# Norm transposes placed inside the next tile, and a first chunk cut by columns at two stage borders

## What is computed

```python
# block 1
x = x + jnp.einsum('ble,ed->bld', mixed, w_out[l])
h = rms_norm(x, ffn_norm_g[l])
g = jnp.einsum('bld,df->blf', h, w_gate[l])
u = jnp.einsum('bld,df->blf', h, w_up[l])
x = x + jnp.einsum('blf,fd->bld', jax.nn.silu(g) * u, w_down[l])
# block 2
x = x + gate1 * (o @ w_o)
h2 = _modulate(x, norm2_g, shift2, scale2)      # rms norm, scale, shift
qp = (h @ w_pq)                                 # 8 heads x 2 halves x 128
sc = jnp.einsum("bshpd,hpnd->bshpn", qp, sub_keys)
# top 16 per half, top 16 of the pairs, then experts from peer_u, peer_v
```

## Time and profile before

| | before |
|---|---|
| median of 3 runs | 2701.93 us |
| lowest, highest | 2696.2, 2707.88 us |
| profiled execution | 2702.28 us |
| its span, first to last instruction | 2700.4 us |
| mean granted TensorE clock | 0.976 |
| TensorE / VectorE / ScalarE / GpSimd busy | 94 / 65 / 35 / 14% of the span |

### The profile page before, as it was taken

The page is one execution under the profiler, slowest core; times in us unless marked ns, Lnnn a source line. Parts: engine busy times, 40 slices in busy tenths (PEclk is TensorE's granted clock), DMA queues, the critical chain, the costliest instruction groups (busy, mean ns, idle before and its releaser), DMA issues.

```text
span 2700.4 us, 37751 instructions
## 1 busy us (share of the span) xinstructions
PE 2527.5 (94%) x13685; PEld 2150.7 (80%) x13685; DVE 1754.7 (65%) x3867; ACT 953.9 (35%) x1695; POOL 366.9 (14%) x326
## 2 busy tenths in 40 slices
PE   8998978999998987989998989999999999999998
PEld 6777777777777955784488988898988989899976
DVE  5535556554325545556899957877878787777755
ACT  4334422222223535521154544333333333333332
POOL 1001110110000000100000002332333333232300
PEclk9999979999999988999999999999999999999999
DMA  4110004663221201022024456887787887787754
GB/s 181 63 47 1 1 1 162 228 234 120 92 94 63 79 32 48 1 79 86 8 71 164 172 221 213 302 289 264 271 284 271 286 274 279 270 287 264 262 187 140
DMA packets 123077, 431.40 MB, mean 160 GB/s; under 512 B 11648, under 2 KB 36480, under 8 KB 110736
## 3 DMA queue, kind: packets, MB, share of 16 engines
q1 hardware_dynamic: 74336, 241.20, 25.9%
q0 software_dynamic: 44064, 160.98, 17.2%
q10 hardware_dynamic: 4496, 26.84, 2.5%
HBM read 399.61 MB, written 29.36 MB: 159 GB/s over the span
## 4 chain that ended last, share of the span: by engine, by line
PE 73%; DVE 16%; ACT 3%; issue 3%; DVEq 2%; DMA 1%; ACTq 1%; POOL 0%; SPq 0%
PE ps L2116 16%; PE ps L2089 14%; PE ps L1883 9%; PE ps L1837 7%; PE ps L1753 5%; PE ps L1905 4%; PE ps L2075 3%; PE ps L1818 2%; PE ps L2149 2%; PE ps L2025 2%; DVE r L1608 1%; PE ps L1790 1%; PE ps L2006 1%; DVE big L1665 1%; ACT r L678 1%
## 5 line engine op out<-in xcount | busy, mean ns | idle before, releaser
L2089 PE MATMUL ps<-hd_hi,uT_hi 128*128 128x384 f32 x1024 | 349.9, 342 | 2.3 <-ACT uT_lo L911 2.3
L2089 PE MATMUL ps<-hd_hi,uT_lo 128*128 128x384 f32 x1024 | 346.5, 338 | 0.0
L2089 PE MATMUL ps<-hd_lo,uT_hi 128*128 128x384 f32 x1024 | 346.3, 338 | 0.0
L2116 PE MATMUL ps<-v_hi,ew_hi 128*128 128x512 f32 x768 | 321.6, 419 | 9.6 <-DVE ew_lo L1581 5.3
L2116 PE MATMUL ps<-v_hi,ew_lo 128*128 128x512 f32 x768 | 305.2, 397 | 0.0
L2116 PE MATMUL ps<-v_lo,ew_hi 128*128 128x512 f32 x768 | 303.3, 395 | 0.0
L1561 DVE TENSOR_TENSOR uT_lo<-ps,uT_hi 128x512 fp32r<-128x512 f32 x204 | 140.8, 690 | 171.9 <-ACT uT_hi L884 166.9
L576 POOL DMA_INDIRECT big<-peer_u,r x128 | 144.9, 1132 | 736.0 <-DVE r L1637 437.1
L884 ACT ACTIVATE uT_hi<-ps 128x512 fp32r<-128x512 f32 x256 | 152.4, 596 | 181.6 <-PE ps L2075 181.6
L2089 PEld LDWEIGHTS ps<-hd_hi,uT_hi 128*128 128x128 f32 x1024 | 192.7, 188 | 11.3 <-ACT uT_lo L911 3.0
L2089 PEld LDWEIGHTS ps<-hd_hi,uT_lo 128*128 128x128 f32 x1024 | 192.6, 188 | 11.0
(11 more groups left out here) (338 smaller groups left out, 5238.4 us busy)
## 6 DMA issues: line engine op xcount, KB each, us to landing
big<-wst SPq DMA_DIRECT2D x70, 1024.0 KB, 4.9
r<-peer_u SPq DMA_DIRECT2D x128, 512.0 KB
r<-peer_v SPq DMA_DIRECT2D x128, 512.0 KB
r<-wada POOLq DMA_DIRECT2D x48, 512.0 KB, 4.7
gd<-big ACTq DMA_DIRECT2D x24, 1024.0 KB, 9.2
big<-gd SPq DMA_DIRECT2D x32, 768.0 KB
x<-x_in SPq DMA_DIRECT2D x4, 512.0 KB, 6.6
xd<-x SPq DMA_DIRECT2D x4, 512.0 KB, 9.9
```

Of the source, the lines that this page charges most:

```text
L2089: mm = pe.matmul(ps[:, acc_bank(j), 0:DN], w[:, k, :], h[:, KD // 2 * half + k, :], start=(half == 0 and k == 0 and i == 0), stop=(half == ...
L2116: mm = pe.matmul(ps[:, 2 + 2 * t + half, :], w[:, P * t:P * t + P], vv[:, 512 * half:512 * half + 512], start=(i == 0 and n == 0), stop=(i ...
```

## The change

In `mixed_linear` TensorE issues the transposes of tile t-1 behind the second of tile t's four blocks, and no longer those of tile 3, which go to the stage behind. VectorE's evacuation moves with them, from behind `scaled(t)` to behind the second addition. The halves of chunk W_GU are made earlier, on ScalarE ahead of tile 2's norm and on VectorE ahead of tile 3's additions.

The first chunk of gate/up is computed in four pieces: columns 0 to 383 (tiles 0 to 2) of gate, then tile 3's norm transposes, columns 0 to 383 of up, and, once tile 3 is evacuated, columns 384 to 511 of gate and of up. The first chunk of the query product is cut likewise into its two query tiles, and the h2 transposes come behind it; the first scores follow those.

```diff
@@ ScalarE, mix_and_norm
+                    if t == T - 1 and not first:
+                        high_part(W_GU)
...
-            high_part(W_GU)
             high_part(W_GU + 1)
@@ VectorE, block 1 (block 2: evac moved alike)
                 if t + 1 < T:
                     mixed_low(0, t + 1, h_lo)
+                else:
+                    low_part(W_GU)
                 for n in range(4):
                     v.wait_ge(out_acc, 4 * t + n + 1)
                     xs = x[:, t, 256 * n:256 * n + 256]
                     v.tensor_tensor(xs, xs, ps[:, 4 + n, 0:256], ALU.add).then_inc(out_add, 1)
+                    if t and n == 1:
+                        evac(t - 1)
                 scaled(t)
-                if t:
-                    evac(t - 1)
-            low_part(W_GU)
             evac(T - 1)
@@ TensorE, mixed_linear
-                    if t:
-                        norm(layer, [t - 1], buf)
-                norm(layer, [T - 1], buf)
+                        if t and n == 1:
+                            norm(layer, [t - 1], buf)
@@ TensorE, gate/up
-            pe.wait_ge(ln_hT, 9)
+            def gate_up(f, u, lo, hi):
+
+                w_parts = [w.rearrange("p (k u n) -> p k u n", k=KD, u=2)
+                           for w in (high_of(W_GU + f), w_lo[:, (W_GU + f) % WR, :])]
+                for k in range(KD):
+                    for i, (w, h) in enumerate(passes(w_parts, (h_hi, h_lo))):
+                        mm = pe.matmul(ps[:, 2 * (f % 2) + u, lo:hi], w[:, k, u, :], h[:, k, lo:hi],
+                                       start=(k == 0 and i == 0), stop=(k == KD - 1 and i == 2))
+                return mm
...
+                if f == 0:
+                    pe.wait_ge(ln_hT, 8)
+                    gate_up(0, 0, 0, DN)
+                    norm(1, [T - 1], xn1)
+                    gate_up(0, 1, 0, DN)
+                    pe.wait_ge(ln_hT, 9)
+                    gate_up(0, 0, DN, T * P)
+                    mm = gate_up(0, 1, DN, T * P)
+                else:
+                    gate_up(f, 0, 0, T * P)
+                    mm = gate_up(f, 1, 0, T * P)
@@ TensorE, queries
+            def queries(c, lo, hi):
+
+                wt = ring[:, (W_PQ + c // 2) % WR, :].rearrange("p (k n) -> p k n", k=KD)
+                for k in range(KD):
+                    mm = pe.matmul(ps[:, c % 4, lo:hi], wt[:, k, P * (c % 2):P * (c % 2) + P], hT[:, k, lo:hi],
+                                   start=(k == 0), stop=(k == KD - 1))
+                return mm
+
+            chunk(pe, W_PQ)
+            pe.wait_ge(ln_hT, 16)
+            queries(0, 0, DN)
+            norm(3, [T - 1], xn4)
+            queries(1, 0, DN)
             pe.wait_ge(ln_hT, 17)
+            for c in range(2):
+                queries(c, DN, T * P).then_inc(qp_acc, 1)
+            pe.drain().then_inc(w_used, 1)
             pe.wait_ge(out_add, 8 * T)
             for k in range(KD):
                 mm = pe.transpose(ps[:, 4 + k // 4, P * (k % 4):P * (k % 4) + P], hT[:, k, DT * P:T * P], ident)
             mm.then_inc(h2_tr, 1)
             pe.wait_ge(subk_in_s, 16)
             for c in range(17):
-                if c < 16:
-                    w = W_PQ + c // 2
-                    chunk(pe, w)
+                if 2 <= c < 16:
+                    chunk(pe, W_PQ + c // 2)
```

More of the change, by code:

```diff
@@ L2037, in _ @@
             for c in range(17):
-                if c < 16:
-                    w = W_PQ + c // 2
-                    chunk(pe, w)
+                if 2 <= c < 16:
+                    chunk(pe, W_PQ + c // 2)
                     if c >= 4:
                         pe.wait_ge(qp_ev, c - 3)
[L2043 to L2047, removed]
+                    queries(c, 0, T * P).then_inc(qp_acc, 1)
                     if c % 2:
```

## The result

The median went from 2704.04 us (6 runs, 2696.2 to 2713.63) to 2683.93 us (6 runs, 2678.0 to 2693.49): ratio 0.9929, 95% interval 0.991 to 0.9948. That is 20.1 us less, where 18.0 were forecast. The execution of after that was profiled is the longest of its six: 2693.49 us, span 2691.6. So the spans of the two pages (2700.4 and 2691.6) say little by themselves; the tails must be read by distances within one trace.

A forecast was written before the change was run, and what follows sets the result against it. TensorE, 73% of the chain that ended last, was taken as the bound, idle at the end of both output projections. Gains of 9.0 + 9.0 = 18.0 us from 2702.3 gave 2684.3 us, range 2680 to 2690.

The forecast's parts named there:

- Tail A: First output projection, last addition to first silu: 25.26 us before, 16.3 after with 0.87 for inserted transposes, gain 9.0.
- 48 narrow matmuls at 0.111: Tail A's single-pass matmuls of 128 columns: 5.35 us in all, with bounds of 0.059 and 0.222 us each.
- rival 2: Narrow single-pass matmuls cost as much as two-pass ones, 0.222 us: gain 12.7, time 2689.6 us, chance 0.09.
- 0.25 put down for changes of stream: Tail A: 0.25 us added to the sum for TensorE's changes of stream.
- thinnest margin: Tail A: tile 3's evacuation is over 0.8 us before TensorE comes to the last columns; a miss costs under a microsecond.
- Tail B: Second output projection, last addition to third query tile: 28.71 us before, 19.7 after, gain 9.0.
- new wait: Tail B: TensorE waits 1.7 us ahead of the first scores for ScalarE's evacuations of h2 and query tile 0.
- Then the first scores, 0.9: Tail B: the first scores behind TensorE's wait for ScalarE take 0.9 us.
- Rival 1: Tail B: the wait ahead of the first scores lets the clock fall; gain 15.8, time 2686.5 us, chance 0.15.
- The sum: Both tails together: 9.0 + 9.0 = 18.0 us off 2702.3, giving 2684.3 us, 0.67% less.
- Rival 3: Work behind tail B doesn't move, so half or all of B's gain is lost: 2689 to 2693 us, chance 0.06.
- Rival 4: Transposes and narrow matmuls among wide ones hold the clock at 1.2 GHz in both tails: 2713 us, chance 0.02.

The follow-up runs named there:

- e1: The whole change measured again against the kernel before: 2686.49 us, ratio 0.9922.
- e4: The whole change at the second projection only, nothing at the first, against the kernel before: 2691.14 us, ratio 0.9947.
- e12: The whole change timed a third time, against the kernel before: 2686.22 us against 2704.71, ratio 0.993.
- e5: The whole change plus two unused 512-column matmuls in the gap behind the h2 transposes, against the kernel before: 2679.54 us, ratio 0.9919.
- e7: e6 with the scores of two query tiles taken together behind each odd query tile, against the kernel before: 2677.98 us, ratio 0.9907.
- e6: The whole change with the h2 transposes ahead of the first query chunk's narrow part, against the kernel before: 2679.24 us, ratio 0.9913.

## Why the prediction was right, and where not

**Tail A** was forecast at 16.3 us and measured 15.07 + 0.87 = 15.9. The term that was a choice, 48 narrow matmuls at 0.111, has its row now: 441.38 to 446.58 are 47 steps, 0.111 each. The bounds of 0.059 and 0.222 both fall, and rival 2 with the latter. The Trainium skill ("TensorE: Matmul & The Clock Gate", Back-to-back issue gap) gives about 81 ns for such a matmul; the trace of after doesn't agree for this single-pass stream, 111 ns. The prediction's reason, the same weight load, fits the traces but wasn't tested: weight loads fill all of the narrow single-pass stretch (4.90 of 4.90 us from 441.50) and all of the narrow two-pass one (3.00 of 3.00 from 1212.20). The other 0.4 us is the 0.25 put down for changes of stream, which doesn't show, and a 48th step, 0.11, where 47 lie between the first start and the last. The thinnest margin was right: tile 3's evacuation ended at 440.6, where the next instruction of VectorE starts, and its columns were asked for at 441.38, 0.8 us later. That ScalarE's exponential of crow (a row of inputs loaded by GpSimd) would wait 2.20 us for its transfer wasn't foreseen; it cost nothing, since the silu behind it waited 5.25 us for TensorE anyway.

**Tail B** was forecast at 19.7 and measured 19.55 + 0.87 = 20.4. The new wait is 1.65 us for a forecast 1.7, by the two evacuations that were named. The step that failed is "Then the first scores, 0.9", a cost taken from a row at full clock: start to start they took 1.48 (1218.46 to 1219.94), 0.6 more, and the query tile behind them 1.16 more, which the forecast to the first top-k also lacked.

**Rival 1 is what happened**, though it had 0.15. The chance was read off, where a gap of 1.62 us kept the clock. That row wasn't read too short: the trace of before has the clock at 1.00 from there to 226 us. But it has matmuls and not transposes ahead of its gap. In after a gap of 1.65 us lost the clock, with eight transposes ahead of it, and all four profiles with this gap (after, e1, e4, e12) show it (scores 1.55 to 1.69 us, query tile 8.19 to 8.34). Behind matmuls a gap of 1.71 to 1.75 us kept it in all 14 profiles of the last stage. So length alone doesn't decide; which of the differences does wasn't tried. Its price was forecast at 2.2 us and is 1.7 by e5. The Trainium skill (same page, Part 4: PE-mode transpose) says that transposes don't count as TensorE being busy in the same way; the outcome, 1.69 us for eight scores instead of 1.05, agrees with what it would give; no run here puts matmuls in the transposes' place, so the rule itself isn't tested.

**The sum** of 18.0 is 16.4 where the trace can be read, 9.3 + 7.1, with A 0.3 above its term and B 1.9 below. The median of the first comparison shows 20.1. By the tails alone the time would be 2702.3 - 16.4 = 2685.9, next to rival 1's 2686.5; the three medians are 2683.93, 2686.49 and 2686.22. That the first one fell on 2684.3 almost exactly is partly luck: B's term was 1.9 too good, and low-clock stretches outside the tails made up for it.

**Rival 3** fell: e4 alone passes its gain on, and the distance from first top-k to first v_high is 366.1 us in after, 366.3 in before. But its kind is what stopped e7: there an earlier top-k met an order written for the later one. Rival 4 fell with the granted clock of 1.00 in tail A and in tail B up to 1215.60; its price was also a little low, as 0.32 and 0.213 us aren't twice 0.175 and 0.111, and doubled in full it comes to some 2716 instead of 2713. The moved steps cost nothing beside the 0.87 us per tail, as forecast; no further wait of TensorE of over 0.3 us stands in either tail.

**Open** is why the medians of the changed kernels lie 2 to 8 us further below before than their tails do. The clock of the runs accounts for most of it, and no wait that the change moved does; why some executions lose the clock at a wait where others keep it, and why the changed kernels lose less, wasn't found.

## What to carry to other kernels

When an engine waits for the last tile of a stage, give it the next stage's work for the tiles that are ready: moving the preparation by itself brought 6.1 us here, the split chunk the other 10.3. A short wait that is left on TensorE can cost as much again in clock (1.65 us of waiting and 1.7 of clock), so look for independent work to put beside it, as e6 does. And where an order is written out by hand, follow a gain made at its head to the next engine that keeps the old places: five of e7's 6.9 us, by the distances in the trace, came back only when two activations were moved.

## What the runs showed of the hardware

A wait of 1.65 us behind eight transposes lost the clock in four profiles of four, one of 1.72 us behind matmuls in none of 14, and one of 2.28 us in some and not in others. In after it still stood at 1.00 (2.4 GHz) over the wait and fell to 0.50 (1.2 GHz) in the work behind it (1218.90 to 1222.00), so a glance at the wait's own slice of the page would have missed it.

Single-pass matmuls hardly get cheaper below 256 columns. The timeline of TensorE in e12 has single-pass matmuls of 256 columns at the end of the second projection, 1195.19 to 1195.55 in three steps of 0.12:

```profile
1195.19 0.28 PE L1839 MATMUL ps<-w_lo,h_hi 128*128 128x256 f32 x1
1195.30 0.28 PE L1839 MATMUL ps<-h_lo,mid 128*128 128x256 f32 x1
1195.42 0.28 PE L1839 MATMUL ps<-h_lo,h_hi 128*128 128x256 f32 x1
1195.55 0.29 PE L1839 MATMUL ps<-w_lo,h_hi 128*128 128x256 f32 x1
```

At 128 columns it is 0.111. An undivided one of 512 columns takes 0.23, by the timeline of after behind the first chunk:

```profile
447.29 0.39 PE L1879 MATMUL ps<-h_hi,w_lo 128*128 128x512 f32 x1
447.52 0.39 PE L1879 MATMUL ps<-h_lo,w_hi 128*128 128x512 f32 x1
447.75 0.39 PE L1879 MATMUL ps<-h_hi,w_hi 128*128 128x512 f32 x1
```

So the split itself cost tail A 48 x (0.175 + 0.111 - 0.23) = 2.7 us, with 0.175 for 384 columns. In tail B, whose matmuls have two passes, it cost nothing (0.32 + 0.11 against 0.43).

Last, a stage of 1090 us with unchanged code varied by 0.6% on TensorE's busy time alone, for the most part by the number of waits that lost the clock. A local gain of 0.3% is better read from distances in the trace than from one median.
